# Scratch stores in runs of 512 tokens, earlier constants, and a new order of masks, square root and copies in the recurrence of an RWKV-7 decoder layer

## The reference

```
proj = rms_norm(x) @ w_in                  # r, k, v, decay, alpha, gate; pooling columns
w, alpha, g, kk, k_mod = ...               # sigmoids, exps, normalised keys
state = state * w_t + (state @ a_t) b_t + v_t k_t     # per head and token
y_t = state @ r_t
y = group_norm(y) * ln_x_w + ln_x_b        # mean, variance, root per head
out = (y + bonus) * g
```

## Time and profile before

| | us |
|---|---|
| runs shown (3) | 2374.41 median, 2373.21 to 2376.77 |
| profiled execution, its own time | 2372.11 |
| its span | 2370.2 |
| project phase | 0 to 563 |
| recur phase | 563 to 901 |
| PE busy | 2212.9 (93%) |
| DVE busy | 1752.8 (74%) |
| ACT busy | 1124.0 (47%) |
| mean granted TensorE clock | 0.959 of full speed |

### The profile page before, as it was taken

The page is one execution under the profiler, slowest core; times in us unless marked ns, Lnnn a source line. Parts: engine busy times, 40 slices in busy tenths (PEclk is TensorE's granted clock), DMA queues, the critical chain, the costliest instruction groups (busy, mean ns, idle before and its releaser), DMA issues.

```text
span 2370.2 us, 39095 instructions
## 1 busy us (share of the span) xinstructions
PE 2212.9 (93%) x14412; PEld 1803.8 (76%) x14412; DVE 1752.8 (74%) x1891; ACT 1124.0 (47%) x1795; POOL 1016.9 (43%) x645
## 2 busy tenths in 40 slices
PE   7989898996877989998999999999999999999998
PEld 6767676774766867886888888888878888887886
DVE  3756597993666554769999999655799888986565
ACT  5646455451343553445444444455554444444543
POOL 5635366560132363544777677200046565641000
PEclk9999999996787989999999999999999999999999
DMA  7374556347454745887343434577743232325774
GB/s 201 97 205 131 146 156 186 103 116 208 106 148 126 204 139 170 267 276 235 111 155 123 147 117 135 190 256 242 257 147 111 88 115 93 114 94 201 249 255 142
DMA packets 480537, 389.03 MB, mean 164 GB/s; under 512 B 108380, under 2 KB 409100, under 8 KB 477068
## 3 DMA queue, kind: packets, MB, share of 16 engines
q1 hardware_dynamic: 430076, 340.96, 47.3%
q10 hardware_dynamic: 50320, 46.14, 6.0%
HBM read 264.87 MB, written 122.16 MB: 163 GB/s over the span
## 4 chain that ended last, share of the span: by engine, by line
PE 53%; DVE 4%; DMA 2%; ACT 2%; issue 1%; SPq 0%; ACTq 0%; POOLq 0%; POOL 0%; DVEq 0%
PE late_bank L133 17%; PE late_bank L134 17%; PE late_bank L135 17%; DMA scratch_a<-p_keep 1%; DVE wt_lo L2866 1%; PE late_bank L2159 1%; ACT wt_hi L2687 1%; DMA o_lo<-scratch_q 0%; DMA p_keep<-in_w_down 0%; ACT late_bank L2705 0%; DMA raw<-in_w_down 0%; DVE wt_lo L2820 0%; DVE p_ub L2900 0%; DMA raw<-in_w_up 0%; DMA p_keep<-scratch_td 0%
## 5 line engine op out<-in xcount | busy, mean ns | idle before, releaser
L133 PE MATMUL late_bank<-o_hi,wt_hi 128*128 128x512 f32 x1232 | 481.0, 390 | 9.6 <-DVE o_lo L2922 3.0
L134 PE MATMUL late_bank<-o_lo,wt_hi 128*128 128x512 f32 x1232 | 480.0, 390 | 0.0
L135 PE MATMUL late_bank<-o_hi,wt_lo 128*128 128x512 f32 x1232 | 479.9, 390 | 0.0
L436 POOL TENSOR_TENSOR p_w_lo<-p_w_raw,p_w_hi 128x1024 fp32r<-128x1024 f32 x72 | 190.7, 2649 | 234.8 <-ACT p_w_hi L495 234.8
L133 PEld LDWEIGHTS late_bank<-o_hi,wt_hi 128*128 128x128 f32 x1232 | 231.6, 188 | 61.0 <-issue 8.2
L135 PEld LDWEIGHTS late_bank<-o_hi,wt_lo 128*128 128x128 f32 x1232 | 231.7, 188 | 48.4
L134 PEld LDWEIGHTS late_bank<-o_lo,wt_hi 128*128 128x128 f32 x1232 | 231.7, 188 | 47.8
L2557 POOL TENSOR_TENSOR tsum<-raw 128x512 f32<-128x512 f32 x43 | 107.0, 2489 | 357.4 <-DVE p_ub L2907 178.2
L133 PE MATMUL p_ppr<-p_hT_hi,p_w_hi 128*128 128x512 f32 x576 | 233.4, 405 | 2.9 <-ACT p_ring L506 2.4
L133 PE MATMUL late_bank<-wt_hi 128*128 128x512 f32 x572 | 223.2, 390 | 6.5 <-DVE wt_lo L2866 5.4
L134 PE MATMUL p_ppr<-p_hT_lo,p_w_hi 128*128 128x512 f32 x576 | 226.1, 392 | 0.0
(11 more groups left out here) (322 smaller groups left out, 4622.6 us busy)
## 6 DMA issues: line engine op xcount, KB each, us to landing
raw<-in_w_up SPq DMA_DIRECT2D x88, 512.0 KB, 5.1
p_w_raw<-in_w_in SPq DMA_DIRECT2D x72, 512.0 KB, 3.9
scratch_a<-p_keep SPq DMA_DIRECT2D x22, 1280.0 KB, 4.5
raw<-scratch_a SPq DMA_DIRECT2D x96, 256.0 KB, 3.0
raw<-scratch_td SPq DMA_DIRECT2D x52, 256.0 KB, 3.6
p_keep<-scratch_a SPq DMA_DIRECT2D x47, 256.0 KB, 3.1
scratch_a<-p_keep SPq DMA_DIRECT2D x44, 256.0 KB, 2.0
raw<-in_w_down SPq DMA_DIRECT2D x44, 256.0 KB, 4.3
```

Of the source, the lines that this page charges most:

```text
L133: nc.tensor.matmul(out, lhs_hi, rhs_hi, start=start, stop=False, skip_group_check=again)
L134: nc.tensor.matmul(out, lhs_hi, rhs_lo, start=False, stop=False, skip_group_check=again)
L135: return nc.tensor.matmul(out, lhs_lo, rhs_hi, start=False, stop=stop, skip_group_check=again)
L436: nc.gpsimd.tensor_tensor(w_lo[i][:, :, :], w_raw[i][:, :, :], w_hi[i][:, :, :].bitcast(F32), ALU.subtract).then_inc(s_wl, 1)
```

## The change

- The scratch arrays become six, `a_`, `r`, `b`, `k`, `bonus`, `g`, each [128, 4, 2048], so that a block's store writes runs of 512 tokens.
- The loads per group of 128 tokens stay in runs of 64 (b, k) and become runs of 128 tokens (a, r, bonus, gate), with two DMAs in place of one for a and r and for bonus and gate: 19 issues a group in place of 17.
- The five constants are loaded at the end of SP's stream in the project phase, behind the first group's operands (now six DMAs).
- DVE: masked(0) moves ahead of the turn of x1 and of the solve parts; then come gap(0), advance(0), the turn of x1, masked(1), gap(1), gap(2).
- ACT: the square root moves from the end of the iteration to the place between m1 and the taking of u(1).
- ACT takes p and u whole, one instruction of 512 columns for a chunk in place of two of 256; PE's inverse runs its 16 matmuls after one wait, with heads interleaved.

```diff
-                    sp.dma_start(kind("ar", b, 1), tokens(um[:, R0:R0 + PAIRS, :])).then_inc(s_rst, 16)
+                    sp.dma_start(scr["r"][:, :, bass.ds(b * TB, TB)], um[:, R0:R0 + PAIRS, :]).then_inc(s_rst, 16)
...
+                for key in ("ident", "strict", "causal"):
+                    sp.dma_start(scr["first_" + key][:, :], const_view(a, key)).then_inc(s_head, 16)
...
-                def store(key, m, src, b, done):
-                    act.dma_start(kind(key, b, m), tokens(src)).then_inc(done, 16)
+                def store(key, src, b, done):
+                    act.dma_start(scr[key][:, :, bass.ds(b * TB, TB)], src).then_inc(done, 16)
...
-                            sp.sem_inc(s_in[0], 80)
-                            for dst, key in ((ident[:, :], "ident"), (strict[:, :], "strict"), (causal[:, :], "causal")):
-                                sp.dma_start(dst, const_view(a, key)).then_inc(s_par, 16)
+                            sp.sem_inc(s_in[0], 96)
+                            sp.sem_inc(s_par, 80)
...
-                            sp.dma_start(rows(ar[n % BATCH]), group("ar", n)).then_inc(s_in[n % 2], 16)
+                            for m, key in enumerate(("a_", "r")):
+                                sp.dma_start(ar[n % BATCH][:, :, m, :], group(key, n)).then_inc(s_in[n % 2], 16)
...
-                        sp.dma_start(rows(bg[n % 2]), group("bg", n)).then_inc(s_in2[n % 2], 16)
+                        for m, key in enumerate(("bonus", "g")):
+                            sp.dma_start(bg[n % 2][:, :, m, :], group(key, n)).then_inc(s_in2[n % 2], 16)
...
                         act.wait_ge(s_as, ONE + i * 2 + c2 + 1)
-                        for h in range(2):
-                            nc.scalar.activation(pz[rows_of(c2), h * PAIRS:(h + 1) * PAIRS, :], pbank[rows_of(c2), h], ACT.Copy).then_inc(s_p, 1)
+                        nc.scalar.activation(pz[rows_of(c2), :, :].rearrange("s (h j) v -> s h j v", h=2), pbank[rows_of(c2)], ACT.Copy).then_inc(s_p, 1)
...
-                        for h in range(2):
-                            act.wait_ge(s_xp, ONE + i * 4 + c2 * 2 + h + 1)
+                        act.wait_ge(s_xp, ONE + i * 2 + c2 + 1)
...
                         take("m1", (m1[:, :, :], blocks))
+                    if c:
+                        act.wait_ge(s_var, ONE + i - 1)
+                        nc.scalar.activation(stat[p][:, 2, :], stat[p][:, 1, :], ACT.Sqrt, scale=1.0 / H, bias=geps[:, 0:1]).then_inc(s_sd, 1)
                     if b:
                         take_u(1)
...
-                    if c:
-                        act.wait_ge(s_var, ONE + i - 1)
-                        nc.scalar.activation(stat[p][:, 2, :], stat[p][:, 1, :], ACT.Sqrt, scale=1.0 / H, bias=geps[:, 0:1]).then_inc(s_sd, 1)
...
                     if a2:
+                        masked(0)
+                    gap(0)
+                    if i == N - 1:
+                        low_w(0)
+                    if b:
+                        advance(0)
+                    if a2:
                         n = i + 1
                         dve.wait_ge(s_xl[n % 2], ONE + (n // 2 + 1) * 160)
...
-                    gap(0)
-                    gap(1)
-                    if i == N - 1:
-                        low_w(0)
-                    if a2:
-                        masked(0)
-                    if b:
-                        advance(0)
                     if a2:
                         masked(1)
+                    gap(1)
...
-                        for h in range(2):
-                            pe.wait_ge(s_p, ONE + i * 4 + c2 * 2 + h + 1)
-                            for j in range(PAIRS):
+                        pe.wait_ge(s_p, ONE + i * 2 + c2 + 1)
+                        for j in range(PAIRS):
+                            for h in range(2):
...
-    scr = {k: scratch(k, (BLOCKS, P, PAIRS, TT, 2, SC)) for k in ("ar", "bg", "bk")}
+    scr = {k: scratch(k, (P, PAIRS, SEQ)) for k in ("a_", "r", "b", "k", "bonus", "g")}
```

More of the change, by code:

```diff
@@ L404, in _ @@
                 sp.wait_ge(s_kst, ONE + 16)
-                for c in range(2):
-                    for m in range(2):
-                        sp.dma_start(scr["first_bk"][:, :, 2 * c + m, :], scr["bk"][0][:, :, 0, m, c * L:c * L + L]).then_inc(s_head, 16)
+                for m, key in enumerate(("b", "k")):
+                    for c in range(2):
+                        sp.dma_start(scr["first_bk"][:, :, 2 * c + m, :], scr[key][:, :, c * L:c * L + L]).then_inc(s_head, 16)
                 sp.wait_ge(s_atst, ONE + 16)
                 sp.wait_ge(s_rst, ONE + 16)
-                sp.dma_start(scr["first_ar"][:, :, :, :].rearrange("p j m t -> p j (m t)"), scr["ar"][0][:, :, 0].rearrange("p j m t -> p j (m t)")).then_inc(s_head, 16)
+                for m, key in enumerate(("a_", "r")):
+                    sp.dma_start(scr["first_ar"][:, :, m, :], scr[key][:, :, 0:SC]).then_inc(s_head, 16)
+                for key in ("ident", "strict", "causal"):
+                    sp.dma_start(scr["first_" + key][:, :], const_view(a, key)).then_inc(s_head, 16)
+                with nc.allow_non_contiguous_dma(reason="per-feature parameters, once"):
+                    for key, name in (("lnw", "ln_x_w"), ("lnb", "ln_x_b")):
+                        sp.dma_start(scr["first_" + key][:, :], a[name][0].rearrange("(t p) -> p t", p=P)).then_inc(s_head, 16)
                 store_rk(BLOCKS - 1)
@@ L540, in gates @@
                     act.wait_ge(s_gr, ONE + b + 1)
-                    store("bg", 1, gate[:, :, :], b, s_gst)
+                    store("g", gate[:, :, :], b, s_gst)
                 def pool_out(b, r, banks):
@@ L3162, in build @@
         with ExitStack() as part:
-            for key, shape in (("bk", [P, PAIRS, 4, L]), ("ar", [P, PAIRS, 2, SC])):
+            for key, shape in (("bk", [P, PAIRS, 4, L]), ("ar", [P, PAIRS, 2, SC]), ("ident", [P, P]), ("strict", [P, L]), ("causal", [P, L]),
+                               ("lnw", [P, PAIRS]), ("lnb", [P, PAIRS])):
                 scr["first_" + key] = part.enter_context(nc.sbuf_tensor("first_" + key, shape, F32))
```

56 lines of the change are left out of this document (24 added, 32 removed).

## The result

The changed kernel takes 2313.75 us (median of 4 runs, 2308.27 to 2317.07), the kernel before 2373.81 beside it: a ratio of 0.9743 with a 95% interval of 0.972 to 0.9765, or 60 us less. The forecast was 2309 in 2288 to 2337.

What follows compares the result with a forecast made beforehand. PE waits for DVE's mask at grams(1) in iterations 0 to 9 and for hT_lo at block boundaries. 21.5 + 2 + 4 + 3.2 + 37.3 - 0.6 - 2 = 65.4 us off 2374.4 gives 2309, range 2288 to 2337.

Steps and rivals of the forecast that it cites:

- Stores: Project phase: ACT's store issues shorten to 0.37 us, cutting PE's block-boundary waits and the phase's end; 27.5 us gained.
- The first rival: Project phase: issue time goes with bytes, not runs, so stores still block ACT; 27.5 us lost, 2336.5; chance 0.12.
- Constants and first iterations: Start of recur phase up to iteration 1: earlier constants and masked(0) gain 3.2 us, between 1.0 and 5.2.
- Masks and root: Recur iterations 2 to 9: wait at grams(1) goes, a 14.5 us wait at to_state(1) comes; 37.3 us less.
- POOL holds the solve parts: Recur phase, DVE: all 46 solve instructions in gap(1) and gap(2) cost 1.31 us, not 0.33; 2354; chance 0.12.
- one meeting an iteration: Iterations 2 to 9: one DVE solve instruction per iteration waits for the POOL pair L1317/L1319 to end, 0.35 us.
- No clock loss: Waits of 1.8 us leave the clock at the upper level and no late tail follows; 2294.6 us; chance 0.12.
- p and u whole: Recur phase, ACT: whole copies cost net 0.1 us an iteration, 0.6 in iterations 10 to 15; bounds 0 and 0.3.
- Loads: Recur phase, SP: two more issues a group cost 0, up to 2 us in iterations 10 to 13.
- Iterations 10 to 14: Recur iterations without solve parts: a change of +0.5 us was forecast for this stretch.
- Tail: Iteration 15: the root waits for the late sum of squares, making u(1) late; +2 us, between 0 and 4.
- Output and MLP: The later phases, not touched by the change: counted as unchanged, 0 us.

Runs made afterwards that it cites:

- the stores alone: The kernel before with only the six scratch arrays, their stores in runs of 512 tokens and their 19 loads a group: 2350.45 us, ratio 0.9897.
- the runs of 256: The changed kernel with scratch arrays laid out so that a block's store writes runs of 256 tokens: 2316.14 us in one run.
- Undoing the stop: The changed kernel with iteration 0's gap(0) moved behind masked(1), from ahead of advance(0): 2304.53 us, ratio 0.9691.
- The single moves: Two kernels, each the changed kernel with one move taken back: square root at iteration's end, 2323.94 us; DVE's old mask order, 2320.49 us.
- the halves: The changed kernel with p and u taken in halves of 256 columns again: 2310.04 us in one run.
- the kernel with both edits: The changed kernel with the sum of squares ahead of gap(1) and gap(2), and iteration 0's gap(0) behind masked(1): 2294.64 us, ratio 0.9643.

## Why the prediction was right, step by step

- **Stores**: -27.1 against -27.5. The wait left at a boundary, 1.7 us, was met. The price of an issue was not: 1.4 us for b and a where I took 0.37 from the pooled store. It didn't matter, since the last issue ends at 133.60 and tile 17's matmuls at 134.99. The precedent was weaker than I took it for: the pooled store is issued by itself, and so is the gate's, which took 0.54 us even in runs of 128 tokens. It could not tell runs from a free queue; the stores alone and the runs of 256 do. The first rival's condition, issues that go with the bytes, is not met for b and a: 10.9 us became 2.8 at the same bytes.
- **Constants and first iterations**: the step that failed. I had seen that advance(0) stands behind the waiting solve instruction and cut the gain to 3.2; 2.4 came. What I had not seen is that half-rate work follows the stop of 2.2 us, in this execution through iteration 1 (+3.5). That 3.5 is not the change's alone: of the seven executions with such a stop, three ran iteration 1 in 12.4 to 12.9 us, like the kernel before, and four in 16.4 to 20.3. Undoing the stop gave 12 us; for the constants themselves no gain is shown. They and the head added six issues to SP's project phase, not the eight that I had counted.
- **Masks and root**: -38.1 against -37.3. The new wait is where I put it, 17.9 us against 14.5; the remainder over 8 x 13.25 us is 6.8 against 10.4 for the clock and 0.8 for the copies. The two errors cancel. The single moves show why both were needed.
- **POOL holds the solve parts** (second rival): in iteration 7 one of the six instructions ahead of the sum took 0.95 us, the other five 0.41. The forecast's one meeting an iteration was right in seven of the eight iterations; each cost about 0.6 us where I took 0.35, since POOL's L1311 (L1319 before) did not end while masked(1) ran.
- **No clock loss** (third rival): half-rate rows follow the waits of 2 to 3 us, as in iteration 7 above.
- **p and u whole**: iterations 10 to 13 grew by 0.04 us in all, against +0.1 each, and the halves show 0.22 an iteration as the price where nothing waits. With solve parts the sign is more likely the other way.
- **Loads**: 0, as forecast, but not with the room that I counted on: 63.2 of SP's 63.6 us of waiting lay in iterations 0 to 9. Behind them SP's loads of a and r came 14.2 us apart in the mean even before the change, PE's iterations 13.24. They are the first thing to wait for once the rest is mended.
- **Iterations 10 to 14**: the 1.8 us won there are not the change's. Before, PE stood still for 0.62 us in iteration 14 with nothing in the profile to wait for, and half-rate work followed; at the same instruction the changed kernel stood 0.32 us, without such work.
- **Tail**: in iteration 15 the sum comes behind 4.51 us of weight splits, and to_state(1) waits 2.20 us where it waited 0.56: +1.6 against +2.

```profile
791.29 4.51 DVE L1497 TENSOR_TENSOR w_lo<-w_raw,w_hi 128x1024 fp32r<-128x1024 f32 x2
...
797.49 1.12 PE L1611 MATMUL late_bank<-p_uv,bkt 128*64 128x64 f32 x16 [2.20 <-ACT p_uv L1342]
```

- **Output and MLP**: I counted 0, and 4.9 us were lost. The kernels profiled here share this code; from the output's first transposes to the end they took between 1459.5 and 1467.0 us. The loss lies in that spread. What sets it was not tried.

So the forecast's 2309 is 5 us under the median; the last point alone would account for it.

## What to carry to other kernels

When a wait is taken from the chain, follow the queue of the engine that ended it to the next instruction that PE needs: here mask, advance(0), sum, root, u(1) stand on two engines, and each place costs as long as any solve part stands in front of it. The work that nobody waits for goes behind all of them: moving the sum and the first step brings another 24 us by the ratios (2294.6). After that SP's issues of the loads decide, so the next step is theirs.

A stop of PE is priced with the half-rate work that follows it, which can be several times the stop. And a price read from a transfer that is issued by itself says little on one that stands behind others.

## What was not expected of the hardware

- A stop of 2.2 to 4.7 us at the start of the phase costs more than itself: the first two iterations take 31.8 to 41.7 us with it, 25.8 to 30.8 without. In the changed kernel TensorE ran at 1.2 GHz (0.5) for 17 us behind it. When the clock comes back differs from execution to execution: 6 us between two executions of one kernel. This bounds what a single run can tell here.
- PE stops now and then without a wait in the profile. In the kernel with both edits, between two rows of one group of matmuls:

```profile
704.04 0.21 PE L1713 MATMUL late_bank<-xd,p_m 32*32 32x32 f32 x1 [1.77 <-issue]
706.63 1.86 PE L1605 MATMUL late_bank<-p_pz,p_xt 64*64 64x64 f32 x15
```

1.77 us of "issue", then half rate (inverse(0)'s 15 in 1.86 us where 1.08 is usual). Between 700 and 706 the DMA engines were 80% busy or more in all but three of 40 slices, and one packet of the instruction queue moved. Most such stops come at a few places: at this last matmul of iteration 9 in six of the kernels profiled (0.3 to 2.3 us), at the 30th of inverse's 32 in iteration 14 in six (0.3 to 1.0). That PE waited for its code there is likely, not shown.
- ACT's issue of a store goes with the run length of the layout where stores follow one another: at 1 MB each, b and a take 10.9, 6.3 and 2.8 us together at 128, 256 and 512 tokens. The gate's store, issued by itself, takes 0.54 at each of the three.
